# HGRN decay levels grouped two by two between two weight slots, in a one-core two-block transformer kernel

## The reference

```python
sig = jax.nn.sigmoid(f_logit)
log_f = jnp.log(lb + (1.0 - lb) * sig)
key = (1.0 - lb) * (1.0 - sig)
...
b = jnp.cumsum(lc, axis=3)
diff = b[:, :, :, :, None, :] - b[:, :, :, None, :, :]
pair_decay = jnp.exp(jnp.where(causal[:, :, None], diff, 0.0))
scores = jnp.einsum('bhnck,bhnsk,bhncsk->bhncs', qc, kc, pair_decay)
scores = jnp.where(causal, scores, 0.0)
o = jnp.einsum('bhncs,bhnsv->bhncv', scores, vc)
```

## Time and profile before

| | |
|---|---|
| median of 3 runs | 1280.37 us (1280.09 to 1280.88) |
| the profiled execution, its own time | 1280.03 us |
| its span, first to last instruction | 1278.2 us |
| around the span | 1.8 us |
| TensorE busy | 1254.3 us, 98% |
| VectorE, ScalarE, GpSimd busy | 820.1, 683.3, 99.4 us |
| mean granted TensorE clock | 0.998 |

### The profile page before, as it was taken

One profiled execution on the slowest core, in us unless ns is written; L12 is line 12 of the kernel. 1 busy time (PEld: TensorE's weight loads), 2 busy tenths in 40 slices (PEclk: granted clock), 3 DMA queues, 4 the chain that ended last, 5 costly groups with the idle time before them and its releaser, 6 DMA issues.

```text
span 1278.2 us, 24816 instructions
## 1 busy us (share of the span) xinstructions
PE 1254.3 (98%) x10520; PEld 1134.0 (89%) x10520; DVE 820.1 (64%) x1241; ACT 683.3 (53%) x885; POOL 99.4 (8%) x81
## 2 busy tenths in 40 slices
PE   6999999999999999999999999999999999999997
PEld 5998899889999999999888888999999999888886
DVE  3667766886856868566655545766868657555543
ACT  2556546865856566245544435766567245544432
POOL 0000000000001320330000000001320230000000
PEclk9999999999999999999999999999999999999999
DMA  9867665624544443235555554444433225555452
GB/s 385 301 252 269 260 227 209 254 77 163 169 148 160 152 133 133 68 101 192 170 197 170 193 197 165 165 137 163 163 133 133 68 99 182 184 178 197 165 186 78
DMA packets 35102, 222.93 MB, mean 174 GB/s; under 512 B 3888, under 2 KB 8240, under 8 KB 9264
## 3 DMA queue, kind: packets, MB, share of 16 engines
q1 hardware_dynamic: 31248, 216.23, 47.9%
q10 hardware_dynamic: 3744, 5.11, 1.2%
HBM read 220.28 MB, written 1.05 MB: 173 GB/s over the span
## 4 chain that ended last, share of the span: by engine, by line
PE 89%; DVE 6%; ACT 2%; DMA 2%; issue 1%; SPq 0%; ACTq 0%; DVEq 0%
PE pj L635 59%; PE yv L635 14%; PE sc L635 9%; PE tp L635 4%; DVE ring_rounded L749 2%; PE tp L501 1%; DMA ring<-weights 1%; PE tp L1940 1%; DMA xT<-x_t 1%; DVE att_area L578 1%; ACT w_split L740 0%; ACT att_area L532 0%; DVE rw L1721 0%; DVE att_area L603 0%; DVE rw L1726 0%
## 5 line engine op out<-in xcount | busy, mean ns | idle before, releaser
L749 DVE TENSOR_TENSOR ring_rounded<-ring,w_split 128x2048 fp32r<-128x2048 f32 x108 | 252.9, 2347 | 59.5 <-ACT w_split L740 57.2
L2166 DVE TENSOR_TENSOR ring_rounded<-ring,big_rounded 128x2048 fp32r<-128x2048 f32 x66 | 151.3, 2292 | 107.8 <-ACT big_rounded L2037 107.7
L740 ACT CAST w_split<-ring 128x2048 fp32r<-128x2048 f32 x106 | 202.2, 1908 | 32.0 <-PE pj L635 22.5
L635 PE MATMUL pj<-h_split,w_split 128*128 128x256 f32 x1264 | 172.4, 287 | 0.2 <-ACT w_split L2416 0.2
L635 PE MATMUL pj<-h_split,ring_rounded 128*128 128x256 f32 x1264 | 165.3, 281 | 1.2 <-DVE ring_rounded L749 1.2
L635 PEld LDWEIGHTS pj<-h_split,w_split 128*128 128x128 f32 x1264 | 156.1, 189 | 7.1 <-issue 5.1
L635 PEld LDWEIGHTS pj<-h_split,ring_rounded 128*128 128x128 f32 x1264 | 155.7, 188 | 2.8 <-DVE ring_rounded L749 2.1
L2037 ACT CAST big_rounded<-ring 128x2048 fp32r<-128x2048 f32 x66 | 126.2, 1912 | 49.9 <-PE pj L635 48.3
L635 PE MATMUL pj<-hT_rounded,w_split 128*128 128x256 f32 x1136 | 146.1, 281 | 0.0
L635 PEld LDWEIGHTS pj<-hT_rounded,w_split 128*128 128x128 f32 x1136 | 139.3, 188 | 0.0
L635 PE MATMUL sc<-big_rounded 128*128 128x512 f32 x176 | 68.8, 391 | 0.0
(11 more groups left out here) (374 smaller groups left out, 2142.0 us busy)
## 6 DMA issues: line engine op xcount, KB each, us to landing
ring<-weights SPq DMA_DIRECT2D x180, 1024.0 KB, 4.9
big<-weights SPq DMA_DIRECT2D x20, 1024.0 KB, 7.8
first_block<-biases ACTq DMA_DIRECT2D x26, 192.0 KB, 4.2
first_block<-biases SPq DMA_DIRECT2D x6, 192.0 KB, 10.9
xT<-x_t SPq DMA_DIRECT2D x1, 1024.0 KB, 9.6
out_t<-scr SPq DMA_DIRECT2D x4, 256.0 KB, 2.9
con<-constants SPq DMA_DIRECT2D x1, 897.0 KB, 6.8
aux<-small SPq DMA_DIRECT2D x1, 832.0 KB, 10.6
```

Source lines behind the costliest of these rows:

```text
L635: return nc.tensor.matmul(out, lhsT, rhs, start=start, stop=stop, skip_group_check=True)
L740: act.post(nc.scalar.copy(w_split[:, w % 2], ring[:, in_ring(idx)]), s["w_high"])
L749: dve.post(nc.vector.tensor_tensor(ring_r[:, at], ring[:, at], w_split[:, w % 2].bitcast(F32), ALU.subtract), s["w_low"])
L2166: dve.tell(nc.vector.tensor_tensor(w_low(t, i), w, value(w_high(i)), ALU.subtract), s["ffn_low"])
```

## The change

The eight steps are put into groups, `TOGETHER = ((0,), (1, 2), (3, 4), (5, 6), (7,))`. Each engine but GpSimd does first the step parts of all steps of a group and then the fill parts:

- TensorE: steps a and b one behind the other, then slot a, the small products beside a, slot b, the small products beside b.
- ScalarE: the exponentials of a and b, then the evacuations and high casts of the two places, with the small work of a and b.
- VectorE: q(a), q(b), then for each of the two its shift, the low part of its slot, its masked copies. Before q(2) there is a wait for the cross product of step 0, whose q buffer it overwrites.
- GpSimd's program is as it was.

No instruction is added or taken away on any engine but that wait.

```diff
+        TOGETHER = ((0,), (1, 2), (3, 4), (5, 6), (7,))
...
+        def pe_hgrn_level(pe, layer, i):
+
+            pe.take(s["hgrn_q"])
+            pe.take(s["hgrn_k"])
...
+            if i > 1:
+                pe.take(s["hgrn_merged"], 2)
+            pe_level((h_bank(i, 0), h_bank(i, 1)), k, q, s["hgrn_scores"])
...
+            for group in TOGETHER:
+                for i in group:
+                    pe_hgrn_level(pe, layer, i)
+                for i in group:
                     fill(pe, pe_slot, f"hgrn{layer}", i)
...
+                    pe_hgrn_beside(pe, layer, i)
...
         def act_hgrn(act, layer):
-            for i, l in enumerate(ORDER):
-                act.take(s["hgrn_diff"])
-                d = flat(h_d[i % 2])
-                act.do(nc.scalar.activation(d, d, ACT.Abs))
-                act.tell(nc.scalar.activation(d, d, ACT.Exp, scale=-1.0), s["hgrn_factor"])
...
-                fill(act, act_slot, f"hgrn{layer}", i - 1)
...
+            for group in TOGETHER:
+                for i in group:
+                    act.take(s["hgrn_diff"])
+                    d = flat(h_d[i % 2])
+                    act.do(nc.scalar.activation(d, d, ACT.Abs))
+                    act.tell(nc.scalar.activation(d, d, ACT.Exp, scale=-1.0), s["hgrn_factor"])
...
+                for i in group:
+                    fill(act, act_slot, f"hgrn{layer}", i - 1)
...
-            for i, l in enumerate(ORDER):
-                if i:
-                    dve_hgrn_q(dve, i)
-                if i < 4:
-                    dve_shift(dve, layer, i)
-                fill(dve, dve_slot, f"hgrn{layer}", i - 1)
...
+            for group in TOGETHER:
+                for i in group:
+                    if i == 2:
+                        dve.eng.wait_ge(s["hgrn_cross"].sem, layer + 1)
+                    if i:
+                        dve_hgrn_q(dve, i)
+                for i in group:
+                    l = ORDER[i]
+                    if i < 4:
+                        dve_shift(dve, layer, i)
+                    fill(dve, dve_slot, f"hgrn{layer}", i - 1)
```

More of the change, by code:

```diff
@@ L1203, in pe_level, with pe_hgrn_beside @@
                             last.then_inc(signal.sem, 1)
+        def pe_hgrn_level(pe, layer, i):
+            pe.take(s["hgrn_q"])
+            pe.take(s["hgrn_k"])
+            q, k = h_upper(i), h_kf[i % 2]
+            if ORDER[i] == LEVELS:
+                for c in range(2):
+                    for r in (0, HD):
+                        last = matmul(tp[r // HD][:, c * P:(c + 1) * P], k[r:r + HD, c, 0:P],
+                                      q[r:r + HD, c * P:(c + 1) * P])
+                last.then_inc(s["hgrn_cross"].sem, 1)
+                return
+            if i > 1:
+                pe.take(s["hgrn_merged"], 2)
+            pe_level((h_bank(i, 0), h_bank(i, 1)), k, q, s["hgrn_scores"])
+        def pe_hgrn_beside(pe, layer, i):
+            if i == 3:
+                pe.take(s["hgrn_crossed"])
+                if layer == 1:
+                    pe.take(s["v_shifted"], 2)
+                    for c in range(2):
+                        last = matmul(tp[1][0:32, 0:SEQ], aux[:, 1, 512 + c * 32:512 + (c + 1) * 32], r_v[:, c],
+                                      c == 0, c == 1)
+                    last.then_inc(s["v_low"].sem, 1)
+            if i == 4 and layer == 1:
+                pe.take(s["v_low_copied"])
+                for c in range(2):
+                    last = matmul(tp[0][:, c * SEQ:(c + 1) * SEQ], aux[0:32, 1, 576 + c * P:576 + (c + 1) * P],
+                                  v_low[0:32])
+                last.then_inc(s["v_mix"].sem, 1)
+            if i == 5:
+                pe.take(s["kk_squares"], 2)
+                pe_head_sums(tp[1], kk_square, s["kk_sums"])
         def pe_hgrn(pe, layer):
@@ L1208, in pe_hgrn @@
             pe_by_half(sc, h_key, hq, s["hgrn_scores"])
-            for i, l in enumerate(ORDER):
[L1210 to L1218, removed]
-                    fill(pe, pe_slot, f"hgrn{layer}", i)
[L1220 to L1241, removed]
+            for group in TOGETHER:
+                for i in group:
+                    pe_hgrn_level(pe, layer, i)
+                for i in group:
+                    fill(pe, pe_slot, f"hgrn{layer}", i)
+                    pe_hgrn_beside(pe, layer, i)
             pe.take(s["hgrn_merged"], 2)
@@ new lines, in act_hgrn @@
+            for group in TOGETHER:
[4 more added lines that the diff above has]
+                    act.tell(nc.scalar.activation(d, d, ACT.Exp, scale=-1.0), s["hgrn_factor"])
+                    if i == 1:
+                        act.take(s["hgrn_cross"])
+                        act.do(nc.scalar.copy(h_scx[:, 0], tp[0][:, 0:SEQ]))
+                        act.tell(nc.scalar.copy(h_scx[:, 1], tp[1][:, 0:SEQ]), s["hgrn_crossed"])
+                for i in group:
+                    fill(act, act_slot, f"hgrn{layer}", i - 1)
+                    if i == 3:
+                        act.take(s["low_shifted"])
+                        act.do(nc.scalar.activation(lora_t[0:HD, 0], r_low[0:HD, 0], ACT.Tanh))
+                        act.do(nc.scalar.activation(lora_t[:, 1], r_low[:, 1], ACT.Tanh, scale=0.5))
+                        act.tell(nc.scalar.activation(lora_t[:, 1], lora_t[:, 1], ACT.Identity, bias=eps[:, 2:3], scale=0.5),
+                                 s["lora_in"])
+                    if i == 4:
+                        act.take(s["k_shifted"])
+                        for c in range(2):
+                            ins = nc.scalar.activation(kk_square[:, c], r_k[:, c], ACT.Square,
+                                                       scale=V("k_k", 2 * layer + c))
+                            if c == 0:
+                                act.post(ins, s["kk_squares"])
+                        act.post(ins, s["kk_squares"])
+                        if layer == 1:
+                            act.take(s["v_low"])
+                            act.post(nc.scalar.copy(v_low[0:32], tp[1][0:32, 0:SEQ]), s["v_low_copied"])
+                    if i == 5 and layer == 1:
+                        act.take(s["v_mix"])
+                        for c in range(2):
+                            act.post(nc.scalar.activation(v_gate[:, c], tp[0][:, c * SEQ:(c + 1) * SEQ], ACT.Tanh,
+                                                          bias=cols[:, 37 + c:38 + c], scale=0.5), s["v_gate"])
@@ new lines, in dve_hgrn @@
+            for group in TOGETHER:
[9 more added lines that the diff above has]
+                    fill(dve, dve_slot, f"hgrn{layer}", i - 1)
+                    if i == 6:
+                        dve.take(s["kk_sums"])
+                        dve.post(nc.vector.tensor_scalar(kk_roots, tp[1][:, 0:8], 1e-24, None, ALU.max), s["kk_floor"])
+                    if i == 4 and layer == 0:
+                        dve.post(nc.vector.tensor_copy(vfirst[:, :, :], r_v), s["v_final"])
+                    if l == LEVELS:
+                        continue
+                    for T in range(NT):
+                        dve.take(s["hgrn_scores"])
+                        n, blocks = 1 << l, P >> (l + 1)
+                        into = flat(h_sc[T]).rearrange("p (h a x n) -> p h a x n", h=NH, x=2, n=n)[:, :, :, 1]
+                        mask = half_of(level(l), n, 1).bitcast(I32).unsqueeze(1).to_broadcast([P, NH, blocks, n])
+                        dve.tell(nc.vector.copy_predicated(into, mask, h_bank(i, T)[:, 0:SEQ].rearrange(
+                            "p (h a n) -> p h a n", h=NH, n=n)), s["hgrn_merged"])
```

## The result

The changed kernel takes 1282.42 us (median of 18 runs, 1280.90 to 1284.07) against 1280.24 (18 runs, 1279.88 to 1281.13): +2.2 us, a ratio of 1.0017 with a 95% interval of 1.001 to 1.0025. It is slower, by less than the 0.2% that I took as the bound. Its runs spread over 3.2 us where those of before spread over 1.3. Two single executions further down, at 1370.96 and 3149.66 us, were disturbed and are left out of the ranges given there.

What follows compares the result with a forecast made beforehand. TensorE, busy 98% of the span and never waiting in layer 0's HGRN steps, was taken as the bound. Lateness +2.7 less savings 1.5 gave +1.2 us: 1280.0 to 1281.2 profiled, 1281.5 as median, range 1278.6 to 1286.0.

Steps and rivals of the forecast that it cites:

- the 0.2% that I took as the bound: Whole kernel: a change under 0.2%, 2.56 us, can hardly be told from none; chance of same 0.68.
- The savings: TensorE, three pairs in two layers: fewer crossings between small and large products save 1.5 us, bounds 1.35 and 2.1.
- the 0.15 I took: TensorE, three pairs with a small product left alone between slots: 0.15 us saved each, 0.45 together.
- the 0.35: TensorE: a second step laid against the first costs 0.94 us in place of 1.29, saving 0.35.
- Step b comes late: Pairs (3, 4) 0.63 us late in both layers, (5, 6) 1.44 in layer 0, none elsewhere; 2.7 together.
- diff(7) runs free if it starts first: GpSimd, pair (5, 6): diff(7) starts before q(6) and takes about 1.1 us instead of 2.97.
- The rival that it stays at 2.97: GpSimd loses the race or late diffs are slow themselves: diff(7) takes 2.97 us, total 1286.0; chance 0.20.
- The low part of slot 3: VectorE, moved at no cost: ready about Z + 11.8, read from Z + 12.1, Z being slot 1's or 3's end.
- the likeliest case: The forecast of 1281.5 us itself, spanning 1279.5 to 1283.5; chance 0.50.

Runs made afterwards that it cites:

- the other order of starts: The change, but VectorE makes the low part of slot 5 between q(5) and q(6), not behind q(6): 1288.85 us, ratio 1.0066.
- key(b) first: The change, but GpSimd does key(b) right behind key(a), and the next pair's two diffs behind both: 1279.76 us, ratio 0.9997.
- The filled wait: The change, plus 3 more TensorE products, result overwritten, in front of step 6 of layer 0: 1281.25 us, ratio 1.0006.
- the squares later: On the kernel with key(b) first, ScalarE's two squares and v_low copy moved behind the exponentials of (5, 6): 1278.94 us, again 1279.05.

## Why the prediction came out as it did

**The savings (1.5 forecast).** Right. Taken pair by pair from the two timelines, without the waits and the slow stretch, they are 0.34, 0.29 and 0.18 us in layer 0 and 0.34, 0.08 and 0.23 in layer 1, 1.46 together; the three pairs with a small product beside them (0.18, 0.08, 0.23) came near the 0.15 I took. Two small errors cancelled in the 0.35, which is luck: the slots between steps run at 1.90 us a third and not at the 1.88 of the plain slot I took, which makes a step's two crossings 0.06 cheaper; but the way from step b into its slot is 0.05 shorter (426.96 to 427.95, 0.99) than from a step that comes out of a slot (1.04), unless b had to wait.

**Step b comes late, GpSimd's order is why (2.7 forecast).** Right in mechanism, a little large. Against the 0.94 spacing, step 4 was 0.41 late in layer 0 (forecast 0.63) and 0.42 in layer 1 (start to start 922.64 to 924.00, forecast 0.63); steps 5 and 6 of layer 0 together 0.2 + 1.17 = 1.4 (forecast 1.44); step 6 of layer 1 nothing (forecast nothing). Sum 2.2. The idle times in the timeline are 0.24 and 1.00 where I had announced 0.6 and 1.1. The error in step 4 is the key's end: key(4) took 0.79 us and ended 0.59 after q(4) (440.79 against 440.20), and I had used key(6)'s 0.72 for all.

**diff(7) runs free if it starts first.** Right: 1.04 us. The rival that it stays at 2.97 held for the other order of starts, and gave 1288.9 rather than my 1286.0, most of the difference being the clock.

**The low part of slot 3.** Right for the change: it is done at 445.36 and read from 445.84, and there is no idle time inside slot 3 or 4. But that room was the lateness of step 4. Where step 4 is on time, in the kernels with key(b) first, the low part is a little late and costs 0.12 us or more a layer, so it was not free, as the prediction had it, but hidden behind a larger wait.

**What failed: a term was missing.** The sum priced a wait of TensorE by its length alone. The step reads "Sum. +2.7 - 1.5 = +1.2 us". The 1.00 us of idle before step 6 also brought the granted clock to its lower level, and slot 5's first third took 1.37 us more, step 6 itself 0.13: 1.5 us, more than the wait. Lateness 2.2, savings 1.5, clock 1.5 make 2.3 (2.27 without rounding); measured are 2.3 in the two stretches and 2.2 in the medians. The filled wait shows the term by itself: 1282.42 to 1281.25, and 1.4 us in layer 0. It also explains the spread: the fastest run of the change, 1280.90, at a mean clock of 0.998, is where the sum without the clock would put it (1280.24 + 0.8), and the mean clock of the runs falls to 0.996 as their time rises. What makes the stretch longer, or makes it come a second time, in the three slowest runs stays open, since only one execution has a timeline.

So the time fell within the likeliest case's own range, 1279.5 to 1283.5, and that is partly luck: a cause worth 1.5 us that the prediction did not have was offset by a third, because its lateness was 0.5 too large. Without the clock the change would have cost 0.8 us and not 2.2.

## What to carry to other kernels

When two steps of a chain are asked for together, look at the engine whose program was not changed: here one diff in front of a key was worth 1.5 us and, through the clock, as much again. Changing GpSimd's order alone took the loss of 2.2 us away (0.9997 of before, 0.9988 to 1.0006), and with the squares later too a small gain was left, at the edge of what the intervals can tell (0.9988, 0.9980 to 0.9997, and again 0.9991, 0.9982 to 1.0000). In this program, where TensorE is 98% busy, a wait had to be priced twice, by its length and by what the clock does behind it; a spread of runs that grows with an edit, and a mean clock that differs between them, were the signs of it. Small products between large ones hide chains as well as costing crossings: before one is moved, ask what it covered.

## What the runs showed of the hardware

- In the profiled executions, 0.78, 1.00 and 1.16 us of idle TensorE were each followed by 3.4 us at the lower clock, and 2.28, 2.92 and 4.03 us by 6.8 us of it; idle times of 0.33 us and less were followed by none. The clock fell 0.8 us after the end of the 1.00 us, 0.9 after the end of the 1.16, 3.1 after the end of the 0.78, and during the idle time itself in the three longest. With the 1.0 us filled by three small products it did not fall.
- The first third of a slot behind a step takes 2.0 us at the upper clock, and took 3.3 to 3.6 where most of it ran at the lower.
- A GpSimd tensor_tensor of 128x512 took 1.04 us where it started first and 2.97 behind VectorE's 128x2048 one; a key of 128x256 0.79 to 1.11, and 2.77 behind the same.
- Two steps of 64-row products laid together took 0.34 us less than with a slot between them (13.52 against 13.86 us from step 1 to step 3), the second one 0.94 us by itself.
